# Where VectorE makes the second half of a weight during attention: behind or ahead of the next minima

## The reference

```python
h = rms_norm(x, g_mix[l])
c_q, c_kv, k_r, qkv_b, qkv_c, gate_logits = jnp.split(h @ w_in[l], IN_SPLITS, axis=-1)
y_a = mla_mixer(c_q, c_kv, k_r, ...)         # 8 heads, 512 x 512 scores, softmax
y_b = dilated_mixer(q_b, k_b, v_b)           # 3 dilations x 4 heads, banded softmax
y_c = neighbourhood_mixer(q_c, k_c, v_c, rpb[l])   # 8 heads, 8 x 16 neighbours, softmax
gates = jax.nn.sigmoid(gate_logits)
x = x + (gates[0] * (y_a @ w_pa[l]) + gates[1] * (y_b @ w_pb[l])
         + gates[2] * (y_c @ w_pc[l])) @ w_o[l]
h = rms_norm(x, g_ffn[l])
x = x + (jax.nn.silu(h @ w1[l]) * (h @ w3[l])) @ w2[l]
```

## Time and profile before

| | |
|---|---|
| median of 3 runs | 3325.08 us (3322.95 to 3326.72) |
| the profiled execution | 3324.35 us, its span 3322.6 us |
| mean granted clock of PE | 0.995 of full speed |
| PE busy | 3257.8 us, 98% of the span |
| DVE, ACT, POOL busy | 1805.0 us (54%), 1309.0 us (39%), 561.5 us (17%) |
| mla of the first layer, 67 to 162 us | PE busy 86.71 of 95.00 us |
| dilated, p = 0, 182 to 262 us | PE busy 76.98 of 80.00 us |
| dilated, p = 1, 284 to 366 us | PE busy 80.73 of 82.00 us |
| neighbourhood, 388 to 482 us | PE busy 88.78 of 94.00 us |

### The profile page before, as it was taken

One profiled execution on the slowest core, in us unless ns is written; L12 is line 12 of the kernel. 1 busy time (PEld: TensorE's weight loads), 2 busy tenths in 40 slices (PEclk: granted clock), 3 DMA queues, 4 the chain that ended last, 5 costly groups with the idle time before them and its releaser, 6 DMA issues.

```text
span 3322.6 us, 38212 instructions
## 1 busy us (share of the span) xinstructions
PE 3257.8 (98%) x15436; PEld 2702.9 (81%) x15436; DVE 1805.0 (54%) x2716; ACT 1309.0 (39%) x1989; POOL 561.5 (17%) x492
## 2 busy tenths in 40 slices
PE   8999999999999999999999999999999999999998
PEld 7777878888887787788888888888888888888887
DVE  6764574544437664655444455554644358974433
ACT  5643453333226533543322333332423238843221
POOL 1320122011002211221110011110211023531101
PEclk9999999999999999999999999999999999999999
DMA  3022223222221112223232322222232322323332
GB/s 134 33 70 71 89 83 117 95 96 95 95 97 63 58 65 73 94 88 102 92 99 97 109 83 83 80 83 95 89 102 90 101 89 89 99 79 102 101 96 83
DMA packets 84994, 295.60 MB, mean 89 GB/s; under 512 B 9425, under 2 KB 11985, under 8 KB 84817
## 3 DMA queue, kind: packets, MB, share of 16 engines
q1 hardware_dynamic: 84816, 293.15, 26.8%
HBM read 291.02 MB, written 2.10 MB: 88 GB/s over the span
## 4 chain that ended last, share of the span: by engine, by line
PE 83%; DVE 8%; ACT 3%; issue 2%; POOL 2%; DMA 1%; SPq 0%; POOLq 0%; DVEq 0%; ACTq 0%
PE bank L312 82%; PE bank L315 2%; DVE wl L555 1%; ACT wh L528 1%; DVE small L1258 1%; POOL u_g L575 1%; DMA raw<-in_wts 1%; ACT c_k L528 1%; DVE m_ptl L555 1%; DVE u_uc L551 0%; DVE m_qf L545 0%; DVE c_kf L545 0%; DVE u_t L551 0%; DVE b_yf L545 0%; DVE c_ptl L555 0%
## 5 line engine op out<-in xcount | busy, mean ns | idle before, releaser
L555 DVE TENSOR_TENSOR wl<-raw,wh 128x1024 fp32r<-128x1024 f32 (+1 forms) x531 | 676.7, 1277 | 851.2 <-ACT wh L528 850.6
L312 PE MATMUL bank<-zh,wh 128*128 128x512 f32 (+1 forms) x2652 | 1031.4, 389 | 15.1 <-ACT zh L528 8.1
L312 PE MATMUL bank<-zl,wh 128*128 128x512 f32 (+1 forms) x2652 | 1022.1, 385 | 3.0 <-DVE zl L558 2.9
L312 PE MATMUL bank<-zh,wl 128*128 128x512 f32 (+1 forms) x2652 | 1022.6, 386 | 0.9 <-DVE wl L555 0.9
L528 ACT ACTIVATE wh<-raw 128x1024 fp32r<-128x1024 f32 (+1 forms) x531 | 556.0, 1052 | 541.4 <-PE bank L312 483.1
L312 PEld LDWEIGHTS bank<-zh,wh 128*128 128x128 f32 x2652 | 502.0, 189 | 116.3 <-ACT zh L528 8.1
L312 PEld LDWEIGHTS bank<-zh,wl 128*128 128x128 f32 x2652 | 501.6, 189 | 105.1 <-DVE wl L555 3.6
L312 PEld LDWEIGHTS bank<-zl,wh 128*128 128x128 f32 x2652 | 501.9, 189 | 98.5 <-DVE zl L558 3.9
L312 PE MATMUL bank<-f_mh,wh 128*128 128x512 f32 (+1 forms) x748 | 285.0, 381 | 0.0
L312 PE MATMUL bank<-f_mh,wl 128*128 128x512 f32 (+1 forms) x748 | 283.4, 379 | 1.2 <-DVE wl L555 1.2
L312 PE MATMUL bank<-f_ml,wh 128*128 128x512 f32 (+1 forms) x748 | 280.8, 375 | 0.0
(11 more groups left out here) (337 smaller groups left out, 4413.4 us busy)
## 6 DMA issues: line engine op xcount, KB each, us to landing
raw<-in_wts SPq DMA_DIRECT2D x529, 512.0 KB, 3.3
c_nb<-in_c_bias SPq DMA_DIRECT2D x16, 384.0 KB, 3.1
x<-in_xT SPq DMA_DIRECT2D x8, 256.0 KB, 6.4
out<-x SPq DMA_DIRECT2D x16, 128.0 KB, 1.9
b_mask<-in_b_mask SPq DMA_DIRECT2D x2, 576.0 KB, 4.5
r_d<-in_decay SPq DMA_DIRECT2D x4, 256.0 KB, 2.7
raw<-in_wts SPq DMA_DIRECT2D x2, 256.0 KB, 3.7
m_t<-in_mla_tab SPq DMA_DIRECT2D x2, 256.0 KB, 4.8
```

The lines of the kernel that those rows point to most:

```text
L312: return self.e.matmul(out, l, r, start=start, stop=stop, skip_group_check=inside)
L555: return self.e.tensor_tensor(out, src, b32(hi), ALU.subtract)
```

## The change

`Splitter` gets `ahead_of(level)`, which is `ahead()` for a level read earlier. In the three vector loops the level is read at the start of an iteration, and the splits are written in the middle, behind the minima and the reciprocal, in place of the end. In `vector_dil` with p = 1 the `acc` of a part whose gate was done earlier goes ahead of the reciprocal. In pass 0 the four values are evacuated in two halves, the second behind the first unit's exponential (ACT) and minima (DVE). In `scalar_nbr` `wh` goes ahead of the copies of queries, keys and gates. The orders on PE, POOL and SP are the same as before; no instruction is added or dropped.

```diff
+    def ahead_of(self, level):
+
+        self.weights(level + 2 - self.lead)
...
@@ vector_mla
     for i in range(38):
+        level = L.level
...
             L.lo(lo, f4(m.bank[turn_bank(j)]), hi).then_inc(*L.tell("lo", "pt", "mla", l, j))
+        L.ahead_of(level)
         if i % 4 == 1 and i < 29:
...
             vector_k_even(L, l, i // 8 + 1)
-        L.ahead()
+    L.ahead()
...
@@ scalar_dil
-        scalar_bv(L, l, 1)
+        scalar_bv(L, l, 1, range(2))
...
             scalar_exp(L, i, m.b_p[i % 2], m.b_p[i % 2], *key)
+        if i == p == 0:
+            scalar_bv(L, l, 1, range(2, 4))
...
@@ vector_dil
-        vector_bv(L, l, 1)
+        vector_bv(L, l, 1, range(2))
...
     L.lead = 0
-    L.ahead()
     for i in range(13):
+        level = L.level
+        new = at(p, i, 1) if p else ()
...
-        for x, n in at(p, i, 1) if p else ():
+        for x, n in new:
             if x == "g":
                 vector_gate(L, l, 0, n)
+            elif ("g", n) not in new:
+                vector_proj(L, l, 0, n)
+        if i == p == 0:
+            vector_bv(L, l, 1, range(2, 4))
...
             vector_div(L, i, *key)
-        for x, n in at(p, i, 1) if p else ():
-            if x == "p":
+        L.ahead_of(level)
+        for x, n in new:
+            if x == "p" and ("g", n) in new:
                 vector_proj(L, l, 0, n)
...
-        L.ahead()
+    L.ahead()
...
```

## The result

| | median | runs |
|---|---|---|
| before, beside it | 3324.57 us | 4, 3322.95 to 3326.72 |
| changed | 3302.30 us | 4, 3299.14 to 3303.02 |

The ratio is 0.9931, with a 95% interval of 0.9914 to 0.9948: faster by 22.3 us. The forecast was 3310, with a range of 3303 to 3320.

A forecast was written before the change was run, and what follows sets the result against it. The prediction took PE, busy 98% of the span, as the bound. Its terms, 6.95 us a layer, 13.9 for two, 14.7 with the clock, off 3324.35 gave 3309.65, with the median's 0.73 rounded in 3310; range 3303 to 3320.

The forecast's parts named there:

- the clock term: Stretches of PE at half clock after long waits: half of one goes with shorter waits, 0.8 us for both layers.
- mla: Attention loop mla: shorter PE waits for m_p, 3.7 us gained a layer, 1.65 of it at the first two places.
- Three or four stretches more than counted: Rival on PE's clock: falls go away with the waits, 1.6 us each, giving 3304 us; chance 0.14 (below 3306).
- The order's sum: Gains from reordering in mla, both dilated passes and neighbourhood attention: 6.95 us a layer, 13.9 for two.
- The neighbourhood attention: Neighbourhood loop: c_ptl and PE 1.35 us earlier, f_g 0.45; net 1.8 us a layer, between 0.5 and 2.3.
- p = 0: First dilated pass: first unit gains 1.4 us, third loses 0.4; net 1.0 a layer, between 0 and 2.
- The one of p = 1: Second dilated pass, third unit: the split goes behind waiting minima, so PE gets its weight 0.8 us late.
- acc: Second dilated pass: acc moves ahead of b_ptl and the reciprocal, so PE's wait for it shrinks, 1.25 us gained.
- POOL held by the split: In mla, the split running beside POOL's multiplication holds it 0.93 us, so PE starts 0.92 us earlier, not 1.87.
- Half the gain: Rival: DVE's own chain takes over in mla, leaving half the sum, 3318 us; chance 0.26.
- Weights late: Rival: dilated and neighbourhood splits behind minima come late, 3332 us if all 22 by 1 us; chance 0.03.
- That the change does nothing at its places: Rival: m_ql, b_yt or b_v sets the time; only acc and part of c_ptl remain, 5 us, 3320; chance 0.03.

The follow-up runs named there:

- e9: The changed kernel with, in mla at the second head's queries, wh one exponential later and the split behind both pairs of minimum and reciprocal; median 3301.09 us.

## Why the prediction was off

- **The step that failed is above all the clock term.** The forecast priced one stretch rightly (1.6 us) but counted half of one, 0.8, for the whole change, and spoke of the range as holding "two each way". Four went. Two of them, in mla, gave nothing back, since PE would have waited there; the other two gave 3.2 us. By the granted clock of all runs it was more: 21 us less at half clock, less the 6.8 of mla's two, make some 6.6 us at 0.46 us each (an estimate); with the order's 17.8 that is 24.4, where the medians of 24 runs of before and eight of the changed kernel are 24.6 apart. The trace of before showed enough to do better: six stretches, each behind a wait of 1.2 to 3.1 us, and the change shortens four of those six waits by 0.9 us or more. Three or four stretches more than counted were among the rivals, at 3304 and with a chance of 0.14.
- **The order's sum was too low as well**: 17.8 for 13.9. The moves were right, three sizes were not, and two lie beyond the bounds that the prediction gave them. The neighbourhood attention gave 2.8 a layer for 1.8 ("between 0.5 and 2.3"): c_ptl 1.9 for 1.35, all of its wait, f_g 0.57 for 0.45, and 0.25 at a later place that was not counted. mla gave 4.5 for 3.7 (4.0 if POOL were not held): the first two places gave 2.1 for 1.65. DVE's chain is the limit at the second, as counted, but its last step is m_ptl behind the split, at 87.83, not POOL's next multiplication. p = 0 gave 1.2 and 1.7 for 1.0, at a place that moves by up to 0.5 from execution to execution.
- **Late weights were counted at one place only.** The one of p = 1 was right (0.84 for 0.8), and so was acc (1.26 for 1.25). Another, 0.5 for wh behind the first layer's attentions, stood in the sum at nothing.
- **POOL held by the split was right**, and shown by e9: 1.66 us beside it, 0.70 without. By the trace m_p (74.41) and the split lie 1.10 us side by side and m_p is held 0.97. The Trainium skill (SBUF — State Buffer, section "SBUF: two separate sides") says that where a VectorE instruction with two SBUF inputs meets a GpSimd one that reads SBUF, the one that starts first has the shared ports for all of its time and the other fully blocks. The trace agrees, but for 0.13 us of m_p's 0.69.
- **The rivals.** Half the gain: DVE's chain does take over at one place in mla, but later than feared. Weights late: two waits of 0.7 and one of 0.5, no more. That the change does nothing at its places: no.

## What to carry to other kernels

When the order on the limiting engine stays the same, match its instructions one by one in the two traces: the difference of their starts is the account of the change, and shows at once which term of a sum was mis-sized. Where the clock falls behind waits, price a change by all the waits that it shortens, not by the one stretch that a comparison happened to show, and take the granted clock of many runs. Then ask of each stretch whether the engine would have waited for another one right behind it: if so, it costs nothing. And before a queue is reordered, ask for each instruction whether its input is complete before the one that it is queued behind: here the gate, not the split, was worth most of what was left.

## What the hardware showed beyond that

Executions of one program differ by several us, in part because the stretches at half clock differ: before had 3320.65 to 3327.53 over 24 runs, with a mean granted clock of 0.993 to 0.996, and the 15 runs at 0.994 took 2.5 us more in the mean than the seven at 0.995. A stretch can follow a wait of 1.2 us and stay away after one of 3.1 us, in the same execution.
